# Turning SwiGLU activations on VectorE and through SBUF transfers in place of TensorE

## The chip, the cores and the metric

One core of one Trainium2 chip runs the whole program in one launch. The metric is device time in microseconds. In the text PE is TensorE, DVE is VectorE, ACT is ScalarE, POOL is GpSimd and SP is SyncE, which here only issues DMAs.

## The reference, cut to what matters

A block of a streaming encoder for 256 tokens of width 2048, all in float32: a feed-forward network (SwiGLU, hidden width 5632), a mixer (a state-space branch and a sparse attention branch), and a second feed-forward network of the same shape. The change touches only the second network:

```python
def _swiglu(x, w1, w3, w2):
    return (jax.nn.silu(x @ w1) * (x @ w3)) @ w2

h = h + 0.5 * g3[:, None, :] * _swiglu(hn, ffn2_w1[l], ffn2_w3[l], ffn2_w2[l])
```

`hn` comes from an RMS norm and a modulation by nine vectors, which are slices of `silu(c) @ w_ada`. The last of these slices, the gate g3, is computed while the second network runs.

## The kernel before, in words

**Units.** Every weight is streamed from HBM in units of 256 rows by 512 columns (`raw`, 512 KB, a ring of four). ACT copies a unit into a rounded high part (`cast`, L880, `w_hi`), DVE subtracts to get the low part (`sub`, L1368, `w_lo`), both in rings of four, and PE runs `unit` (L2149): 12 matmuls of 512 columns, for two halves of tokens, two slices of 128 rows and three products (high by high, low by high, high by low).

**Blocks.** The hidden width is cut into 11 blocks of 512 columns. In the steady state (`hidden`) a block has 24 units, called unit 0 to unit 23 here: eight of w1 for the next block, eight of w2 for this block (four quarters of the output, two units each), eight of w3 for the next block. The second network begins with 24 units of mixed order, then `second` (16 units, the block o = 0), then `hidden` for o = 1, three trips of a loop over two blocks each (o = 2 to 7), `hidden` for o = 8, and a closing part with o = 9 and 10.

**The activation of a block.** PE leaves x @ w1 and x @ w3 in PSUM with tokens on the partitions. ACT takes the silu (`silu`), DVE multiplies (`prod`, L1588, at unit 2) into `act_tok`. The product with w2 needs the hidden columns on the partitions, so PE turns `act_tok` with eight 128x128 transposes into PSUM (`turn_act`, L2176, just before unit 5). ACT copies that out as `aT_hi` (`act_hi`, L979, after its cast of unit 7), DVE subtracts to get `aT_lo` (`act_lo`, L1590, after its subtraction of unit 7), and PE uses both from unit 8 on.

**What sets the order.** Every engine's stream is written out by hand and runs in order; semaphores tie them together. SP's order is one load per unit (`load_unit`, L650, which waits until DVE has subtracted the unit four before it). During units 20 to 58 of the second network, SP also loads 32 pieces of `w_ada` (512 KB each, `load_ada`, L656), four for every five units, and DVE adds each into `ada_acc` (`ada_add`, L1376, L1388) right after the subtraction of the unit with which it was loaded; after the 16th and the 32nd piece DVE folds the sum (`fold`, L1395, four transposes and four reductions). In this stretch lie `second` (units 24 to 39, called block 0 here) and the first `hidden` (from unit 40, called block 1). DVE also adds each output quarter into `y` (`y_add`, L1595).

Of the kernel before, what the change touches and what calls it, by code (L numbers as in the profile page):

```python
# [26 lines left out]
ALU = mybir.AluOpType  # L27
# [32 lines left out]
FOLD = 32  # L60
FOLD_COLS = 256
LOOP_FROM = (4, 2)
TRIPS = tuple((FBLK - 1 - o) // 2 - 1 for o in LOOP_FROM)
ADA_MIX = ADA_FIRST + ADA_PEELED[0] + ADA_TRIP * (TRIPS[0] + 1)
ADA_MIXED = 3
# [50 lines left out]
def build(nc, x, c, positions, w_ada, b_ada, norm_ffn1, ffn1_w1, ffn1_w3, ffn1_w2, norm_mix, w_in,  # L116
# [77 lines left out]
    act_tok = place("act_tok", at_temp + 24 * KB, [HALF, NB])  # L194
    aT_hi = place("aT_hi", at_temp + 28 * KB, [4, T], F32R)
    aT_lo = place("aT_lo", at_temp + 32 * KB, [4, T], F32R)
    aT2_hi = place("aT2_hi", at_temp + 56 * KB, [4, T], F32R)
    aT2_lo = place("aT2_lo", at_temp + 60 * KB, [4, T], F32R)
    norm_tmp = place("norm_tmp", at_temp + 20 * KB, [2, 2, T])
# [99 lines left out]
    silu_ready = sem("silu_ready")  # L299
    prod_ready = sem("prod_ready")  # L300
    act_turned = sem("act_turned")
    ahi_ready = sem("ahi_ready")
    alo_ready = sem("alo_ready")
    y_added = sem("y_added")
# [194 lines left out]
    def set_of(m):  # L499

        return max(e for e in range(SETS) if SET_START[e] <= m)

    BLOCK = 3 * UPB
    SECOND = 2 * UPB
    PEELED = (len(EARLY), FIRST + SECOND + BLOCK)
# [7 lines left out]
    def rows_cols(w, row, cols):  # L513

        return w[row:row + 2 * P, cols].rearrange("(k p) n -> p k n", p=P)

    def span(start, size):
        return slice(start, start + size) if isinstance(start, int) else bass.ds(start, size)
# [123 lines left out]

    as2 = lambda t: t.rearrange("p (k n) -> p k n", k=2)

    block = ctx.enter_context(nc.Block())


    @block.sync
    def _(sp):
# [6 lines left out]
        def load_ada(m, source):  # L656
# [2 lines left out]
                sp.wait_ge(ada_used, free)  # L659
            sp.dma_start(ada_row(slot), source).then_inc(ada_in[slot], 16)  # L660


        sp.dma_start(h[:], x[0].rearrange("(s p) d -> p s d", p=P)).then_inc(x_in, 16)
        for u in range(LATE[0]):
# [3 lines left out]
        for f in range(2):  # L668
# [5 lines left out]
            for u, source in enumerate(peeled):  # L674
                if f or u >= LATE[0]:
                    load_unit(At(n + u), source)
                i = ada_unit_after(f, u)
                if i is not None:
                    e, k = divmod(i, KT)
                    e += (ADA_FIRST, ADA_FFN2)[f]  # L680
                    if f and i == 0:
                        sp.wait_ge(unit_done, n)
                    load_ada(At(e * KT + k), ada_source(e, k))
            with sp.Fori(0, TRIPS[f]) as trip:
                pair_of_blocks = [source for e in range(2) for source in ffn_sources(f, False, trip * 2 + (LOOP_FROM[f] + e))]
                for u, source in enumerate(pair_of_blocks):
                    load_unit(At(n + PEELED[f] + u, BODY, trip), source)
                    k = ada_unit_after("trip", u)
                    if f == 0 and k is not None:
                        e = ADA_FIRST + ADA_PEELED[0]  # L690
                        load_ada(At(e * KT + k, ADA_TRIP * KT, trip), ada_source(trip * ADA_TRIP + (e + k // KT), k % KT))
            pair_of_blocks = ffn_sources(f, False, FBLK - 3) + closing_sources(f)
            for u, source in enumerate(pair_of_blocks):
                load_unit(At(n + PEELED[f] + TRIPS[f] * BODY + u), source)
                k = ada_unit_after("trip", u)
                if f == 0 and k is not None:
                    e = ADA_MIX - ADA_TRIP + k // KT
                    load_ada(At(e * KT + k % KT), ada_source(e, k % KT))
            if f == 1:
                break  # L700
            for n in range(MIX, M0):
# [146 lines left out]
    def _(act):  # L848
# [126 lines left out]
        def silu(o, bank=0):  # L975
            act.wait_ge(prod_ready, o.count()) if o.n0 else None
            nc.scalar.activation(silu_a[:], psum[:, bank:bank + HALF, :], ACT.Silu).then_inc(silu_ready, 1)

        def act_hi(o, bank=4, dst=aT_hi):  # L979
            act.wait_ge(act_turned, o.count(plus=1))  # L980
            nc.scalar.activation(dst[:], psum[:, bank:bank + 2, :].rearrange("p b (k t) -> p (b k) t", k=2),
                                 ACT.Copy).then_inc(ahi_ready, 1)

# [25 lines left out]
        def ffn(f):  # L1009
            n0 = ffn_base[f]  # L1010
            o0 = f * FBLK
            if f == 0:
                early()
            else:
                cast_units(n0 + W1_DONE + LAG)
                act.wait_ge(unit_done, n0 + W1_DONE)
                silu(At(o0))

            def second(n, o):

                for u in range(SECOND):
                    cast_units(n.n0 + u + 1)
                    if u == 4:
                        act.wait_ge(unit_done, n.n0)
                        silu(o + 1, FIRST_BANK[2])
                    if u == 7:
                        act_hi(o, 0)

            def hidden(n, o):

                for u in range(BLOCK):
                    if n.per:
                        cast(n + u)
                    else:
                        cast_units(n.n0 + u + 1)
                    if u == 7:
                        act_hi(o)
                    if u == UPB - 1 + LAG:
                        act.wait_ge(unit_done, (n + UPB).count())
                        silu(o + 1)  # L1040

            if f:
                second(At(n0 + FIRST), At(o0))
                hidden(At(n0 + FIRST + SECOND), At(o0 + 1))
            with act.Fori(0, TRIPS[f]) as trip:
                for e in range(2):
                    hidden(At(n0 + PEELED[f] + e * BLOCK, BODY, trip), At(o0 + LOOP_FROM[f] + e, 2, trip))
            done[0] = n0 + PEELED[f] + TRIPS[f] * BODY
            hidden(At(done[0]), At(o0 + FBLK - 3))
            n, o = done[0], o0 + FBLK - 2  # L1050
            for u in range(2 * UPB):
                cast_units(n + u + 1)
                if u == 7:
                    act_hi(At(o))
                if u == UPB - 1 + LAG:
                    act.wait_ge(unit_done, n + UPB)
                    silu(At(o + 1))
            n += 2 * UPB
            cast_units(n + 5)
            act_hi(At(o + 1), 0, aT2_hi)  # L1060
            cast_units(n + 6)
            gate_copy(2 * f)
            if f == 1:
                cast_units(n + 2 * UPB)
                return
            close_tail(1, n)
# [295 lines left out]
    def _(dve):  # L1362
# [219 lines left out]
        def prod(o, n, bank=2):  # L1582

            dve.wait_ge(unit_done, n.count())
            dve.wait_ge(silu_ready, o.count(plus=1))
            if o.n0:
                dve.wait_ge(act_turned, o.count())
            nc.vector.tensor_tensor(act_tok[:], silu_a[:], psum[:, bank:bank + HALF, :], ALU.mult).then_inc(prod_ready, 1)  # L1588

        def act_lo(o, bank=4, hi=aT_hi, lo=aT_lo):  # L1590
            dve.wait_ge(ahi_ready, o.count(plus=1))
# [50 lines left out]
        def ffn(f):  # L1642
# [10 lines left out]
            def second(n, o, adds):  # L1653

                for u in range(SECOND):
                    sub_units(n.n0 + u + 1)
                    ada_peeled(f)
                    if u == 2:
                        prod(o, n)
                    if u == 7:  # L1660
                        act_lo(o, 0)
                    if u == 10:
                        prod(o + 1, n + UPB, 4)
                    if u in (12, 14):
                        q = (u - 12) // 2
                        y_add(adds + q, q, n + (UPB + 2 * q + 2), SECOND_BANKS)
# [12 lines left out]
            def hidden(n, o, adds, w0=0, ada=None, after_second=False):  # L1679


                for u in range(BLOCK):
# [10 lines left out]
                        y_add(At(Y_ADDS[f] + q), q, n + (2 * q + 2 - UPB), SECOND_BANKS)  # L1693
                    if u == 2 and not after_second:
                        prod(o, n)
                    if u == 7:
                        act_lo(o)
                    if u in (12, 14, 16, 18):
                        q = (u - 12) // 2
                        y_add(adds + q, q, n + (UPB + 2 * q + 2))  # L1700
# [14 lines left out]
            for u in range(2 * UPB):  # L1715
# [2 lines left out]
                    later_set(BLOCK + u, piece)  # L1718
                if u == 2:
                    prod(At(o), At(n))  # L1720
                if u == 7:
                    act_lo(At(o))
            n += 2 * UPB
            sub_units(n + 2)
            prod(At(o + 1), At(n))
# [419 lines left out]
    def _(pe):  # L2145
# [199 lines left out]
        def ffn(f):  # L2345
# [12 lines left out]
            def second(n, o, adds):  # L2358

                for u in range(UPB):  # L2360
                    if u == 5:
                        turn_act(o, 0)
                    unit(n + u, xT_hi, xT_lo, 2 * u, 4, u == 0, u == UPB - 1)
                for q in range(QB):
                    if q == 0:
# [9 lines left out]
            def hidden(n, o, adds, after_second=False):  # L2375
# [3 lines left out]
                if after_second:  # L2379
                    pe.wait_ge(y_added, (adds + -2).count())  # L2380
                for u in range(UPB):
                    if u == 5:

                        if adds.n0:
                            pe.wait_ge(y_added, adds.count())
# [2 lines left out]
                for q in range(QB):  # L2388
                    bank = 6 if q % 2 == 0 else 4
                    if q == 0:  # L2390
                        pe.wait_ge(alo_ready, o.count(plus=1))
                    if q >= 2:
                        pe.wait_ge(y_added, (adds + (q - 1)).count())
                    for k in range(2):
# [16 lines left out]
            n, o, adds = n + BLOCK, o + 1, adds + QB  # L2411
            pe.wait_ge(silu_ready, o + 1)
            for u in range(UPB):
                if u == 5:
                    pe.wait_ge(y_added, adds)
                    turn_act(At(o))
                unit(At(n + u), xT_hi, xT_lo, 2 * u, 0, u == 0, u == UPB - 1)
# [3 lines left out]
            for i, (block, q) in enumerate(CLOSING):  # L2421
                last = block == FBLK - 1
                hi, lo = (aT2_hi, aT2_lo) if last else (aT_hi, aT_lo)
                if i == 0:
                    pe.wait_ge(alo_ready, o + 1)
                if i == 1:
                    turn_act(At(o + 1), 0)
                    sum_folds(2 * f, 3)
# [334 lines left out]
```

## Time and profile before

| | us |
|---|---|
| median of three runs | 2528.01 |
| the three runs | 2526.07, 2528.01, 2530.00 |
| span of the profiled execution | 2528.3 |
| PE busy | 2499.9 |
| DVE busy | 1830.6 |
| ACT busy | 1159.0 |

No time of its own is given for the profiled execution beside its span; the span is taken for it. A duration in the trace is from an instruction's start to its recorded end; matmuls overlap, so for PE the distance between starts is what counts. DVE and ACT instructions overlap by about 0.1 us as well. DMA issues are shown on the queue of the engine that issues them (SPq, ACTq).

### The profile page before, as it was taken

Reading aid. Unit: us, or ns where it says so; the run is one execution under the profiler, and the core shown is the slowest. Engines: PE = TensorE matmul, PEld = TensorE weight load, DVE = VectorE, ACT = ScalarE, POOL = GpSimd, SP = SyncE. Lnnn points to the kernel's source line nnn. Section 1 sums busy time; section 2 is a strip of 40 time slices with the busy share of each in tenths; the row PEclk is TensorE's granted clock in tenths of the full one; section 3 lists DMA queues with packets and bytes.
Section 4 is the critical chain, followed back from the end, with each engine's and each line's share of the span. In section 5 each row is a group of like instructions: output and inputs, shape, how many; then the busy total and the mean of one; then the engine's idle time right before and its main releaser. Section 6 shows DMA issues by size and latency. Waiting matters only on the chain.

```text
span 2528.3 us, 33298 instructions
## 1 busy us (share of the span) xinstructions
PE 2499.9 (99%) x12314; PEld 2108.9 (83%) x12314; DVE 1830.6 (72%) x2016; ACT 1159.0 (46%) x1396; POOL 84.0 (3%) x118
## 2 busy tenths in 40 slices
PE   7999999999999999999999999999999999999999
PEld 5778888888888999898888888888888888888887
DVE  6876668898877888887866677776689555555556
ACT  4444444444445555655555444444544444444443
POOL 4210000000000000000100000000000000000000
PEclk9999999999999999999999999999999999999999
DMA  9976579898976777874544778787598655565565
GB/s 370 366 282 194 184 261 344 291 341 291 340 259 210 270 261 268 279 228 152 164 142 138 245 267 272 251 298 243 167 334 301 203 192 190 189 191 188 190 191 173
DMA packets 281219, 614.45 MB, mean 243 GB/s; under 512 B 23586, under 2 KB 24196, under 8 KB 280196
## 3 DMA queue, kind: packets, MB, share of 16 engines
q1 hardware_dynamic: 269600, 571.41, 67.4%
q0 software_dynamic: 9744, 36.73, 3.9%
q10 hardware_dynamic: 1748, 4.62, 0.5%
q8 instruction: 80, 1.31, 0.2%
q14 instruction: 47, 0.39, 0.0%
HBM read 608.43 MB, written 4.25 MB: 242 GB/s over the span
## 4 chain that ended last, share of the span: by engine, by line
PE 95%; DVE 2%; DMA 1%; issue 0%; ACT 0%; ACTq 0%; DVEq 0%
PE psum L2159 27%; PE psum L2161 27%; PE psum L2160 27%; PE psum L2453 3%; PE psum L2455 3%; PE psum L2454 3%; PE psum L2476 2%; PE psum L2147 2%; DMA raw<-in_ffn_w 1%; DVE w_lo L1368 1%; PE psum L2269 0%; DVE ada_acc L1482 0%; DMA badas<-in_b_ada 0%; PE psum L2240 0%; PE psum L2201 0%
## 5 line engine op out<-in xcount | busy, mean ns | idle before, releaser
L1368 DVE TENSOR_TENSOR w_lo<-raw,w_hi 128x1024 fp32r<-128x1024 f32 x850 | 1036.6, 1223 | 518.8 <-ACT w_hi L880 517.6
L880 ACT ACTIVATE w_hi<-raw 128x1024 fp32r<-128x1024 f32 x850 | 899.0, 1060 | 1017.4 <-PE psum L2161 873.5
L2159 PE MATMUL psum<-w_hi,xT_hi 128*128 128x512 f32 x1984 | 784.8, 396 | 6.4 <-issue 4.6
L2161 PE MATMUL psum<-w_hi,xT_lo 128*128 128x512 f32 x1984 | 773.8, 390 | 0.0
L2160 PE MATMUL psum<-w_lo,xT_hi 128*128 128x512 f32 x1984 | 773.5, 390 | 0.0
L2159 PEld LDWEIGHTS psum<-w_hi,xT_hi 128*128 128x128 f32 x1984 | 373.1, 188 | 89.8 <-issue 13.1
L2161 PEld LDWEIGHTS psum<-w_hi,xT_lo 128*128 128x128 f32 x1984 | 372.9, 188 | 78.9
L2160 PEld LDWEIGHTS psum<-w_lo,xT_hi 128*128 128x128 f32 x1984 | 373.2, 188 | 75.8
L2159 PE MATMUL psum<-w_hi,aT_hi 128*128 128x512 f32 x704 | 274.8, 390 | 0.0
L2161 PE MATMUL psum<-w_hi,aT_lo 128*128 128x512 f32 x704 | 274.1, 389 | 0.0
L2160 PE MATMUL psum<-w_lo,aT_hi 128*128 128x512 f32 x704 | 274.0, 389 | 0.0
L1388 DVE SCALAR_TENSOR_TENSOR ada_acc<-ada_raw,cact,ada_acc 128x1024 f32<-128x1024 f32 x210 | 268.9, 1280 | 0.0
L2453 PE MATMUL psum<-xT_hi,w_hi 128*128 128x256 f32 x640 | 182.2, 285 | 0.1
L2455 PE MATMUL psum<-xT_hi,w_lo 128*128 128x256 f32 x640 | 181.1, 283 | 0.0
L2454 PE MATMUL psum<-xT_lo,w_hi 128*128 128x256 f32 x640 | 181.1, 283 | 0.0
L2161 PEld LDWEIGHTS psum<-w_hi,aT_lo 128*128 128x128 f32 x704 | 132.1, 188 | 27.6
L2159 PEld LDWEIGHTS psum<-w_hi,aT_hi 128*128 128x128 f32 x704 | 132.2, 188 | 27.4
L2160 PEld LDWEIGHTS psum<-w_lo,aT_hi 128*128 128x128 f32 x704 | 132.2, 188 | 27.2
L1604 DVE TENSOR_TENSOR y<-psum,y 128x1024 f32<-128x1024 f32 x89 | 108.8, 1222 | 22.2 <-PE psum L2161 22.2
L2453 PEld LDWEIGHTS psum<-xT_hi,w_hi 128*128 128x128 f32 x640 | 122.8, 192 | 0.5 <-issue 0.5
L2454 PEld LDWEIGHTS psum<-xT_lo,w_hi 128*128 128x128 f32 x640 | 122.8, 192 | 0.0
L2455 PEld LDWEIGHTS psum<-xT_hi,w_lo 128*128 128x128 f32 x640 | 122.8, 192 | 0.0
(260 smaller groups left out, 1904.6 us busy)
## 6 DMA issues: line engine op xcount, KB each, us to landing
raw<-in_ffn_w SPq DMA_DIRECT2D x528, 512.0 KB, 4.5
ada_raw<-in_w_ada SPq DMA_DIRECT2D x224, 512.0 KB, 5.7
raw<-in_w_in SPq DMA_DIRECT2D x224, 512.0 KB, 3.8
ada_raw<-in_w_ada POOLq DMA_DIRECT2D x32, 512.0 KB, 7.4
ada_more<-in_w_ada POOLq DMA_DIRECT2D x32, 512.0 KB, 7.3
raw<-in_w_br_ssd SPq DMA_DIRECT2D x32, 512.0 KB, 5.3
raw<-in_w_br_att SPq DMA_DIRECT2D x32, 512.0 KB, 4.5
raw<-in_w_out SPq DMA_DIRECT2D x32, 512.0 KB, 5.1
```

The costliest lines, as they stand in the source:

```text
L880: nc.scalar.activation(w_hi[:, n.slot(SPLIT), 0:size], raw[:, n.slot(RAW), 0:size], ACT.Copy).then_inc(hi_ready, 1)
L1368: nc.vector.tensor_tensor(w_lo[:, n.slot(SPLIT), 0:size], raw[:, n.slot(RAW), 0:size], w_hi[:, n.slot(SPLIT), 0:size], ALU.subtract).then_ ...
L1388: nc.vector.scalar_tensor_tensor(out=acc[:], in0=src, scalar=cact[:, k:k + 1], in1=acc[:], op0=ALU.mult, op1=ALU.add).then_inc(ada_used, 1)
L1604: nc.vector.tensor_tensor(y[:, :, cols], psum[:, bank:bank + HALF, :], y[:, :, cols], ALU.add).then_inc(y_added, 1)
L2147: return nc.tensor.transpose(dst, src, ident[0:rows_, 0:rows_])
L2159: nc.tensor.matmul(o, hi[:, kt + k, toks], whi, start=a, stop=False)
L2160: nc.tensor.matmul(o, hi[:, kt + k, toks], wlo, start=False, stop=False)
L2161: ins = nc.tensor.matmul(o, lo[:, kt + k, toks], whi, start=False, stop=b)
L2453: nc.tensor.matmul(o, w_hi[:, s, cols], xT_hi[:, kt + k, :], start=a, stop=False, skip_group_check=True)
L2454: nc.tensor.matmul(o, w_hi[:, s, cols], xT_lo[:, kt + k, :], start=False, stop=False, skip_group_check=True)
L2455: ins = nc.tensor.matmul(o, w_lo[:, s, cols], xT_hi[:, kt + k, :], start=False, stop=b, skip_group_check=True)
L2476: return nc.tensor.matmul(o, a, b, start=first, stop=last)
```

## The change: what it does

For the blocks o = 0 to 9 of the second network PE no longer turns the activations. DVE transposes `act_tok` in 32x32 pieces within each group of 32 partitions (`turn_bands`, two instructions, one for each half of the tokens), right after `prod`. SP waits for that and issues 16 transfers from SBUF to SBUF, 32 partitions by 1 KB each (`move_act`), which carry each 32-partition band to its place. In SP's stream they stand after the loads of unit 6. ACT and DVE then split `aT_raw` into high and low parts as before, each in two instructions (`moved_hi`, `moved_lo`), at the places where `act_hi` and `act_lo` stood. In the first network and in the last block nothing changes.

```diff
+BLOCKED_FROM = (10, 0)
+BLOCKED = tuple(FBLK - 1 - o for o in BLOCKED_FROM)
+BANDS = P // 32
+BAND_DMAS = BANDS * BANDS
...
+    MOVE_AFTER = 6
...
+        def move_act(o):
+
+            sp.wait_ge(act_blocked, moves_before(o).count(plus=1))
+            for band in range(BANDS):
+                for to in range(BANDS):
+                    sp.dma_start(aT_raw[32 * to:32 * (to + 1), band, :],
+                                 act_blk[32 * band:32 * (band + 1), to, :]).then_inc(act_moved, 16)
...
                 for u, source in enumerate(pair_of_blocks):
...
+                    if blocked(o) and u % BLOCK == MOVE_AFTER:
+                        move_act(o)
...
+        def moved_hi(o, n):
+
+            act.wait_ge(act_moved, moves_before(o).count(plus=1) * 16 * BAND_DMAS)
+            act.wait_ge(unit_done, n.count())
+            for half in range(HALF):
+                ins = nc.scalar.activation(by_tokens(aT_hi, half), by_bands(half), ACT.Copy)
+            ins.then_inc(ahi_ready, 1)
...
+        def turn_bands(o):
+
+            dve.wait_ge(prod_ready, o.count(plus=1))
+            for half in range(HALF):
+                ins = nc.vector.transpose(act_blk[:].rearrange("p c (k s t) -> p s k c t", s=HALF, t=32)[:, half],
+                                          act_tok[:, half, :].rearrange("p (k c t) -> p k c t", c=BANDS, t=32))
+            ins.then_inc(act_blocked, 1)
+
+        def moved_lo(o):
+
+            dve.wait_ge(ahi_ready, o.count(plus=1))
+            for half in range(HALF):
+                ins = nc.vector.tensor_tensor(by_tokens(aT_lo, half), by_bands(half), by_tokens(aT_hi, half), ALU.subtract)
+            ins.then_inc(alo_ready, 1)
...
                     if u == 2:
                         prod(o, n)
+                        turn_bands(o)
                     if u == 7:
-                        act_lo(o, 0)
+                        moved_lo(o)
...
             def second(n, o, adds):
 
                 for u in range(UPB):
-                    if u == 5:
-                        turn_act(o, 0)
...
-                    if u == 5:
+                    if u == 5 and not blocked(o):
 
                         if adds.n0:
                             pe.wait_ge(y_added, adds.count())
...
                         pe.wait_ge(alo_ready, o.count(plus=1))
+                        if blocked(o) and adds.n0:
+                            pe.wait_ge(y_added, adds.count())
```

## Rows read from the trace of the kernel before

**Rows 1.** The page's first and fourth parts: busy time of PE, chain by engine.
```profile
PE 2499.9 (99%) x12314; PEld 2108.9 (83%) x12314; DVE 1830.6 (72%) x2016; ACT 1159.0 (46%) x1396; POOL 84.0 (3%) x118
PE 95%; DVE 2%; DMA 1%; issue 0%; ACT 0%; ACTq 0%; DVEq 0%
```

**Rows 2.** Two stretches of the second network: length, busy us by engine, PEclk, DMA share, GB/s.
```profile
1873.00:1960.00 87.00, 87.00 (x392) 72.19 (x391) 81.62 (x82) 36.84 (x35) 0.00 (x0) 1.00 0.86 307
...
2050.00:2460.00 410.00, 410.00 (x1836) 340.06 (x1835) 224.05 (x186) 170.89 (x163) 0.00 (x0) 1.00 0.60 190
```

**Rows 3.** Timeline of PE, one block behind the loads of w_ada: start, duration, instruction.
```profile
2101.79 0.39 PE L2159 MATMUL psum<-w_hi,xT_hi 128*128 128x512 f32 x1
...
2115.16 0.39 PE L2161 MATMUL psum<-w_hi,xT_lo 128*128 128x512 f32 x1
2115.39 1.03 PE L2147 MATMUL psum<-ident,act_tok 128*128 128x128 f32 x8
...
2116.50 0.40 PE L2160 MATMUL psum<-w_lo,xT_hi 128*128 128x512 f32 x1
```

**Rows 4.** Timelines of DVE and ACT in the same block.
```profile
2102.17 1.22 DVE L1588 TENSOR_TENSOR act_tok<-silu_a,psum 128x1024 f32<-128x1024 f32 x1 [0.58 <-PE psum L2161]
2103.31 1.22 DVE L1368 TENSOR_TENSOR w_lo<-raw,w_hi 128x1024 fp32r<-128x1024 f32 x1
...
2112.87 1.06 ACT L880 ACTIVATE w_hi<-raw 128x1024 fp32r<-128x1024 f32 x1 [1.66 <-PE psum L2161]
```

**Rows 5.** DVE's transposes in 32x32 pieces, line 1406.
```profile
L1406 DVE STREAM_TRANSPOSE fold_tmp<-ada_acc x56: 435/440/450, 416.2 to 1951.9; 128x256 f32<-128x256 f32 x56
```

**Rows 6.** Timeline of ACT's DMA queue: shortest, longest, first and last of four small loads.
```profile
6.97 0.97 ACTq L853 DMA_DIRECT2D vecs<-in_ssd_norm  x1
...
9.05 0.23 ACTq L853 DMA_DIRECT2D vecs<-in_k_norm  x1
...
186.25 0.46 ACTq L886 DMA_DIRECT2D a_exp<-in_ssd_a_log  x1
...
187.71 0.46 ACTq L892 DMA_DIRECT2D pos_col<-in_positions  x1
```

**Rows 7.** SP's loads, line 654: 2050 to 2500 us, then landing in 1810 to 1950.
```profile
L654 SPq DMA_DIRECT2D raw<-in_ffn_w x162: 367/373/382, 2053.9 to 2498.0; - x162
DMA to landing us min/median/max: 3.3/4.3/7.0
...
DMA to landing us min/median/max: 3.4/5.4/8.5
```

**Rows 8.** Timeline of DVE in block 0.
```profile
1860.28 1.22 DVE L1588 TENSOR_TENSOR act_tok<-silu_a,psum 128x1024 f32<-128x1024 f32 x1
...
1868.36 1.23 DVE L1368 TENSOR_TENSOR w_lo<-raw,w_hi 128x1024 fp32r<-128x1024 f32 x1 [1.07 <-ACT w_hi L880]
...
1871.09 1.23 DVE L1368 TENSOR_TENSOR w_lo<-raw,w_hi 128x1024 fp32r<-128x1024 f32 x1 [0.30 <-ACT w_hi L880]
...
1874.59 1.23 DVE L1592 TENSOR_TENSOR aT_lo<-psum,aT_hi 128x1024 fp32r<-128x1024 f32 x1 [1.08 <-ACT aT_hi L981]
```

**Rows 9.** Timeline of DVE from the end of block 0 through block 1.
```profile
1898.58 2.35 DVE L1368 TENSOR_TENSOR w_lo<-raw,w_hi 128x1024 fp32r<-128x1024 f32 x2
...
1907.30 1.22 DVE L1604 TENSOR_TENSOR y<-psum,y 128x1024 f32<-128x1024 f32 x1
...
1920.81 1.22 DVE L1368 TENSOR_TENSOR w_lo<-raw,w_hi 128x1024 fp32r<-128x1024 f32 x1
...
1924.70 1.23 DVE L1368 TENSOR_TENSOR w_lo<-raw,w_hi 128x1024 fp32r<-128x1024 f32 x1 [0.34 <-ACT w_hi L880]
...
1928.12 1.23 DVE L1368 TENSOR_TENSOR w_lo<-raw,w_hi 128x1024 fp32r<-128x1024 f32 x1 [1.01 <-ACT w_hi L880]
...
1953.87 4.62 DVE L1368 TENSOR_TENSOR w_lo<-raw,w_hi 128x1024 fp32r<-128x1024 f32 x4
```

**Rows 10.** Timeline of PE: the first matmul of block 1.
```profile
1903.27 0.39 PE L2159 MATMUL psum<-w_hi,xT_hi 128*128 128x512 f32 x1
```

More of the change, by code:

```diff
@@ L196, in build @@
     aT_lo = place("aT_lo", at_temp + 32 * KB, [4, T], F32R)
+    act_blk = place("act_blk", at_temp + 64 * KB, [BANDS, UNIT // BANDS])
+    aT_raw = place("aT_raw", at_temp + 68 * KB, [BANDS, UNIT // BANDS])
     aT2_hi = place("aT2_hi", at_temp + 56 * KB, [4, T], F32R)
@@ L301, in build @@
     act_turned = sem("act_turned")
+    act_blocked = sem("act_blocked")
+    act_moved = sem("act_moved")
     ahi_ready = sem("ahi_ready")
@@ L515, in rows_cols, with blocked, moves_before, turns @@
         return w[row:row + 2 * P, cols].rearrange("(k p) n -> p k n", p=P)
+    def blocked(o):
+        f, i = divmod(o.n0, FBLK)
+        return BLOCKED_FROM[f] <= i < FBLK - 1
+    def moves_before(o):
+        f = o.n0 // FBLK
+        return o + (-BLOCKED_FROM[0] if f == 0 else BLOCKED[0] - FBLK - BLOCKED_FROM[1])
+    def turns(o):
+        before = sum(1 for i in range(o.n0) if not blocked(At(i)))
+        return At(before) if blocked(o) else o + (before - o.n0)
     def span(start, size):
@@ L643, in build, with by_tokens, by_bands @@
     as2 = lambda t: t.rearrange("p (k n) -> p k n", k=2)
+    def by_tokens(t, half):
+        return t[:, :, half * P:(half + 1) * P].rearrange("p k (b t) -> p k b t", t=32)
+    def by_bands(half):
+        return aT_raw[:].rearrange("p b (k s t) -> p s k b t", s=HALF, t=32)[:, half]
     block = ctx.enter_context(nc.Block())
@@ L683, in _ @@
                     load_ada(At(e * KT + k), ada_source(e, k))
+                for i, at in enumerate((FIRST, FIRST + SECOND)):
+                    if f and u == at + MOVE_AFTER:
+                        move_act(At(f * FBLK + i))
             with sp.Fori(0, TRIPS[f]) as trip:
@@ L691, in _ @@
                         load_ada(At(e * KT + k, ADA_TRIP * KT, trip), ada_source(trip * ADA_TRIP + (e + k // KT), k % KT))
+                    o = At(f * FBLK + LOOP_FROM[f] + u // BLOCK, 2, trip)
+                    if blocked(o) and u % BLOCK == MOVE_AFTER:
+                        move_act(o)
             pair_of_blocks = ffn_sources(f, False, FBLK - 3) + closing_sources(f)
@@ L698, in _ @@
                     load_ada(At(e * KT + k % KT), ada_source(e, k % KT))
+                o = At(f * FBLK + FBLK - 3 + u // BLOCK)
+                if blocked(o) and u % BLOCK == MOVE_AFTER:
+                    move_act(o)
             if f == 1:
@@ L977, in silu @@
             nc.scalar.activation(silu_a[:], psum[:, bank:bank + HALF, :], ACT.Silu).then_inc(silu_ready, 1)
+        def moved_hi(o, n):
[4 more added lines that the diff above has]
+            ins.then_inc(ahi_ready, 1)
         def act_hi(o, bank=4, dst=aT_hi):
-            act.wait_ge(act_turned, o.count(plus=1))
+            act.wait_ge(act_turned, turns(o).count(plus=1))
             nc.scalar.activation(dst[:], psum[:, bank:bank + 2, :].rearrange("p b (k t) -> p (b k) t", k=2),
@@ L1026, in second @@
                     if u == 7:
-                        act_hi(o, 0)
+                        moved_hi(o, n)
             def hidden(n, o):
@@ L1036, in hidden @@
                     if u == 7:
-                        act_hi(o)
+                        moved_hi(o, n) if blocked(o) else act_hi(o)
                     if u == UPB - 1 + LAG:
@@ L1053, in ffn @@
                 if u == 7:
-                    act_hi(At(o))
+                    moved_hi(At(o), At(n)) if blocked(At(o)) else act_hi(At(o))
                 if u == UPB - 1 + LAG:
@@ L1585, in prod @@
             dve.wait_ge(silu_ready, o.count(plus=1))
-            if o.n0:
-                dve.wait_ge(act_turned, o.count())
+            if o.n0 and not blocked(o + -1):
+                dve.wait_ge(act_turned, turns(o).count())
             nc.vector.tensor_tensor(act_tok[:], silu_a[:], psum[:, bank:bank + HALF, :], ALU.mult).then_inc(prod_ready, 1)
+        def turn_bands(o):
[9 more added lines that the diff above has]
+            ins.then_inc(alo_ready, 1)
         def act_lo(o, bank=4, hi=aT_hi, lo=aT_lo):
@@ L1695, in hidden @@
                         prod(o, n)
+                    if u == 2 and blocked(o):
+                        turn_bands(o)
                     if u == 7:
-                        act_lo(o)
+                        moved_lo(o) if blocked(o) else act_lo(o)
                     if u in (12, 14, 16, 18):
@@ L1720, in ffn @@
                     prod(At(o), At(n))
+                    if blocked(At(o)):
+                        turn_bands(At(o))
                 if u == 7:
-                    act_lo(At(o))
+                    moved_lo(At(o)) if blocked(At(o)) else act_lo(At(o))
             n += 2 * UPB
@@ L2413, in ffn @@
             for u in range(UPB):
-                if u == 5:
+                if u == 5 and not blocked(At(o)):
                     pe.wait_ge(y_added, adds)
@@ L2425, in ffn @@
                     pe.wait_ge(alo_ready, o + 1)
+                    if blocked(At(o)):
+                        pe.wait_ge(y_added, adds)
                 if i == 1:
```

## The prediction, written before the change was run

> **What bounds the kernel now.** I read the page's busy line and the chain of waits first. The reader is to see that PE is busy for 99% of the span and makes 95% of the chain [rows 1]: whatever PE no longer does is time, as long as nothing makes it wait. Then two stretches of the second network [rows 2]. From 2050 to 2460 us PE is busy all the time, DVE 55%, ACT 42%, the DMA engines 60%: there is room beside PE. From 1873 to 1960 us, where w_ada is loaded too, DVE is busy 81.62 of 87 us and DMA 0.86 of the time. PE does not wait there either, but there is hardly room for more. The granted clock is 1.00 in both, the 2.4 GHz level, and the change gives no reason for another: PE keeps running.
>
> **What is removed.** A unit takes PE (2115.39 - 2101.79) / 5 = 2.72 us; two matmuls start 0.227 us apart. Around the eight transposes, the second matmul behind them starts at 2116.50, where 2115.16 + 2 x 0.227 = 2115.61 would be due without them [rows 3]. So they cost 0.89 us, less than the 1.03 us that the row records for them, since matmuls overlap. Ten blocks: **-8.9 us**. All of it lies on PE's path.
>
> **What is added on DVE.** The nearest row is the transpose of 128x256 in 0.44 us [rows 5]; 1024 columns of another operation take 1.22 us [rows 4], which makes 1.0 ns a column and 0.18 fixed. A half of 128x512 lies between one such transpose (0.44) and two (0.88); I take 0.70. The next instruction starts 0.08 us before the last one's end [rows 4], but the first transpose waits for prod's end. From prod's start: transposes at 1.25 and 1.87, end at 2.57, the next subtraction at 2.49 in place of 1.14, so 1.35 us later. The low part in two halves costs 0.1 more. 1.45 us a block (0.9 to 1.8).
>
> **What is added on SP, the term that decides.** SP waits for the transposes, then issues 16 transfers before the load of unit 7. No row shows such an issue. A lone load of 512 KB takes 0.37 us [rows 7]; four small loads in a row on ACT's queue take 0.46 us each and start 0.49 apart (187.71 - 186.25 over three) [rows 6], so a small one is not cheaper. The shortest issue seen took 0.23 us, the longest 0.97, both at the start, while other queues load as well [rows 6]; these are the two ends, and with 0.97 the 16 would take 15.5 us. I take 0.49, the rows of the same pattern on an otherwise steady queue: 16 x 0.49 = 7.84 us in which no weight is loaded. Behind the wait on SP stands every later load, and for these wait ACT's casts, then DVE, then PE. The transfers themselves have until the cast of unit 7 and land beside the load behind them. The Trainium skill has another price: DMA: Bandwidth & Descriptors, section Anatomy of one DMA, SWDGE (gpsimd) path, gives about 50 ns for the sequencer's dispatch of a DMA. That is for GpSimd's path, and the rows show nine times as much; by it SP would be held for 0.8 us, and the sum would be near the first rival's.
>
> **The eight plain blocks (2 to 9).** Time from unit 0 on PE (2101.79). prod starts at 0.38 [rows 3, 4], the transposes are done at 2.95, the load of unit 7 is issued at 3.0 + 7.84 = 10.8. It lands 3.3, 4.3 or 7.0 us later (least, median, most [rows 7]); the queue has run empty by then, so I expect 3.3 to 4.3: 15.1. The cast (1.06) and subtraction (1.23) end at 17.4. PE wants unit 7 at 7 x 2.72 = 19.0: **1.6 us spare**. Before, the cast of unit 7 started at 11.1, so this is where 4 us of slack go. The high part, in two halves of at most 0.6 us each, takes ACT until 17.4, the low part DVE until 18.7, and the subtraction of unit 8 ends at 19.9, wanted at 21.8. The loads of units 8 to 10 follow 0.49 apart, and SP has caught up by unit 11. Cost 0; if a landing takes above 5.9 us, what is over. The new wait for y_added before unit 8 is three units later than the old one before unit 5: nothing.
>
> **Blocks 0 and 1, where w_ada is loaded.** Here DVE's lateness carries on. Block 1 begins on PE at 1903.27 [rows 10], so block 0 at 1903.27 - 16 x 2.72 - 0.89 = 1858.9.
> - Block 0: prod at 1860.28 [rows 8], transposes done at 1862.9, load of unit 7 at 1870.75, landed (3.4, the least of this stretch [rows 7], since the queue is empty) at 1874.15, cast until 1875.2. DVE was free at 1870.9 and idles for 4.35 us, where before it idled 1.07 + 0.30 + 1.08 [rows 8]. Subtraction, w_ada piece (1.2) and low part follow, and unit 8 is 3.1 us later than before. Some 0.5 us of small gaps are won back. Then come the 16th piece and the fold, the point at which DVE was latest before: the subtraction of unit 15 ended at 1899.8 [rows 9], and PE wanted it at 1900.55. Now it ends at 1902.4, wanted at 1899.66: PE waits **2.7 us**.
> - Block 1 starts on PE at 1905.1. DVE's addition of unit 2 is at 1907.30 + 2.6 [rows 9], the transposes end at 1912.4, the subtraction of unit 3 at 1913.5, wanted at 1913.25: **0.3**. The load of unit 7 is issued at 1920.3, landed at 1923.7, subtracted at 1926.0, wanted at 1924.4: **1.6**. With a w_ada piece and the low part between, unit 8 ends at 1929.6, wanted at 1928.7: **0.9**. DVE is now 7.6 us late against before (1928.4 for 1920.81 [rows 9]) and wins back 0.34 + 1.01 of idle. At the last fold, unit 19 ended at 1955.05 and was wanted at 1955.86; now 1961.25, wanted at 1955.86 - 1.78 + 5.5 = 1959.6: **1.65**.
> Together PE waits 7.1 us. With the stretch's later landings (4.3 in place of 3.4) it is 8.9; each 0.1 us more or less per issue moves it by 3.2; the bounds of the transposes by 1 either way.
>
> **The sum.** -8.9 + 7.1 = -1.8 against the profiled execution's 2528.3, which is 0.3 above the median of the runs shown: **2526.5 us**, or 0.07% less. A measurement of this kernel tells about 0.2%, 5 us, from no change. So the forecast is: most of what PE gains in ten blocks is lost in two.
>
> **Rivals.**
> 1. *The gain comes through.* If an issue takes 0.23 us, the lower end, the load of unit 7 is 4.2 us earlier and DVE hardly waits for it; DVE's own 1.45 us fit into the idle 2.45 of block 0, and in block 1 only unit 3 is late: it ended at 1909.66, now 1911.2, wanted at 1910.5, 0.7 us. -8.9 + 0.7: **2520.1**. For it: a lone issue is shorter than one in a row [rows 6, 7], and SP is not ACT. At 0.40 us per issue the loss is 4.2 and the time 2523.6. Against: four issues in a row agree to 0.01 us.
> 2. *The loads are late in all blocks.* One mechanism: the stop of SP's queue eats the spare 1.6 us of the plain blocks. It decides from 7.84 + 1.6 = 9.4 us for the 16 transfers, 0.59 us each (or landings above 5.9). At 0.65 us: 1.0 us in each of eight blocks, and 7.1 + 2 x 2.6 = 12.3 in blocks 0 and 1: -8.9 + 8 + 12.3 = +11.4, **2539.7**. For it: 16 outstanding transfers behind one another are shown nowhere, and landings of 7.0 occur. Against: it takes a fifth more than the rows' 0.49. At the upper end of 0.97 the spare time would be overrun by 6.1 us a block and the time be near 2590; I give that 0.03.
> 3. *Between:* 0.49 us per issue, but landings at the medians in both stretches, the transposes at their upper bound: 7.1 + 1.8 + 1 = 9.9, a net +1.0: 2529.3, slower but not measurably.
>
> **How the numbers follow.** The forecast and what lies within 5 us of the time before, rival 3 included: 0.47. Rival 1 down from 0.38 us per issue: 0.33. Rival 2 and its like: 0.20, the upper end's 0.03 included. The range reaches to the first rival's end and halfway to the second's: 2519.5 to 2534.
>
> **What would show it.** Transposes of 128x512 near 0.70 us. SP's 16 issues spanning 7.8 us, and the load of unit 7 at 10.8 us behind unit 0. In the plain blocks ACT's cast of unit 7 waits for a DMA at about 15 us, PE not at all, and a block takes 24 x 2.72 = 65.3 us. PE waits for w_lo in two places of each of the blocks 0 and 1, some 7 us in all, where it hardly waited before. The prediction is wrong if the issues are not 0.45 to 0.55 us apart, or if PE waits in the plain blocks.

## The result, and the profile after

| | before | after |
|---|---|---|
| median, us | 2528.69 | 2542.45 |
| runs, us | 2526.07 to 2530.00 (4) | 2539.79 to 2544.06 (4) |
| profiled execution: time, span | 2530.00, span 2528.3 | 2539.79, span 2538.1 |

Ratio 1.0055, 95% interval 1.0041 to 1.0069: the changed kernel is slower by 0.55%, 13.8 us. The forecast was 2526.5, the range ended at 2534. In every run for which both are known the span is 1.7 us shorter than the time, so the profiled execution of the kernel before is its slowest run, 2530.00, and that of the changed kernel is its fastest. The two profiles therefore differ by only 9.8 us.

PE's and DVE's busy time and the chain by engine on the page, which answer to [rows 1]:

```profile
PE 2495.9 (98%) x12234; PEld 2100.3 (83%) x12234; DVE 1841.8 (73%) x2046; ACT 1158.4 (46%) x1406; POOL 83.8 (3%) x118
PE 85%; DVE 5%; SPq 4%; DMA 3%; issue 2%; ACT 1%; ACTq 0%; DVEq 0%
PE psum L2236 23%; PE psum L2238 23%; PE psum L2237 23%; SPq L700 4%; PE psum L2532 3%; PE psum L2534 3%; PE psum L2533 3%; DMA raw<-in_ffn_w 3%; PE psum L2555 2%; PE psum L2224 2%; DVE w_lo L1425 2%; DVE ada_acc L1445 1%; ACT w_hi L929 1%; DVE act_tok L1645 0%; PE psum L2346 0%
```

PE is busy 4.0 us less, only 1.5 of it in the second network (729.27 and 727.75). The 8.9 us of transposes are gone, but matmuls at half clock, of which more below, count as busy longer. And the chain now runs through SP's queue: L700, the line that issues the transfers, has 4% of it, 100 us, which is ten blocks of 10 us.

The pieces that were added (name, engine, operation, count, ns min/median/max, first and last start):

```profile
L700 SPq DMA_DIRECT2D aT_raw<-act_blk x160: 512/590/1528, 1859.9 to 2454.9; - x160
L1651 DVE STREAM_TRANSPOSE act_blk<-act_tok x20: 668/688/712, 1858.5 to 2444.8; 128x512 f32<-128x512 f32 x20
L1033 ACT ACTIVATE aT_hi<-aT_raw x20: 611/614/617, 1875.3 to 2461.1; 128x512 fp32r<-128x512 f32 x20
L1659 DVE TENSOR_TENSOR aT_lo<-aT_raw,aT_hi x20: 682/684/689, 1877.8 to 2462.4; 128x512 fp32r<-128x512 f32 x20
```

The transposes take 0.69 us (forecast 0.70). An issue takes 0.59, and in a plain block SP stands at its transfers for 10 us. SP's and ACT's timelines in the block that begins on PE at 2112.23:

```profile
2109.47 3.09 SPq L686 DMA_DIRECT2D raw<-in_ffn_w  x2
2115.12 10.04 SPq L700 DMA_DIRECT2D aT_raw<-act_blk  x16
2125.46 0.38 SPq L686 DMA_DIRECT2D raw<-in_ffn_w  x1
```

```profile
2129.18 1.06 ACT L929 ACTIVATE w_hi<-raw 128x1024 fp32r<-128x1024 f32 x1 [7.53 <-DMA raw<-in_ffn_w]
2130.15 1.14 ACT L1033 ACTIVATE aT_hi<-aT_raw 128x512 fp32r<-128x512 f32 x2
2131.80 1.06 ACT L929 ACTIVATE w_hi<-raw 128x1024 fp32r<-128x1024 f32 x1 [0.52 <-DMA raw<-in_ffn_w]
```

SP reaches the transfers 2.9 us behind PE's unit 0, as forecast, and the load of unit 7 13.2 us behind it, where 10.8 was forecast. ACT waits 7.53 us for that load and casts at 16.9; with the cast (1.06) and DVE's subtraction (1.23) the unit is ready at 19.2, and PE wanted it at 19.0. The spare time is gone, by a little.

In blocks 0 and 1 it is more than a little. Who waited for whom from 1850 to 1982 us (engine, line, released by: us in all, times, longest):

```profile
ACT w_hi L929 <- DMA raw<-in_ffn_w: 57.0, 28, 11.2
DVE w_lo L1425 <- ACT w_hi L929: 24.8, 13, 8.2
...
PE psum L2236 <- DVE w_lo L1425: 9.7, 5, 3.8
PE psum L2236 <- DVE y L1676: 1.4, 1, 1.4
```

Read from top to bottom they are one chain: the load is late, so ACT, so DVE, so PE. PE is held up before units 7, 8, 12 and 15 of block 0 (some 2.0, 0.9, 1.6 and 2.5 us) and before units 7 and 19 of block 1 (some 4.1 and 1.6). PE's timeline at the end of block 0 shows what else happened (the first two rows; then block 1 begins), and two windows give the granted clock (length, busy us of PE, PEld, DVE, ACT, POOL, then PEclk, DMA share, GB/s):

```profile
1903.52 0.50 PE L2236 MATMUL psum<-w_hi,aT_hi 128*128 128x512 f32 x1 [2.20 <-DVE w_lo L1425]
...
1904.92 0.63 PE L2237 MATMUL psum<-w_lo,aT_hi 128*128 128x512 f32 x1
...
1907.96 0.40 PE L2236 MATMUL psum<-w_hi,xT_hi 128*128 128x512 f32 x1
```

```profile
1904.10:1907.50 3.40, 3.40 (x10) 2.62 (x9) 3.40 (x5) 0.00 (x0) 0.00 (x0) 0.50 0.84 276
1931.40:1934.80 3.40, 3.40 (x10) 2.62 (x9) 3.40 (x5) 1.31 (x2) 0.00 (x0) 0.50 1.02 392
```

PE waited 2.2 us for a low part, and soon after it went on its clock was granted at 0.50 (1.2 GHz) for 3.4 us: matmuls start 0.43 us apart in place of 0.227. The same follows the longest wait of block 1, 3.8 us. Each stretch costs 1.7 us more. Before, the clock was 1.00 in this stretch [rows 2]. The four runs of the changed kernel differ in this: their mean clocks are 0.998, 0.997, 0.997 and 0.996 as their times rise from 2539.79 to 2544.06, and the profiled one is the fastest.

**Where the time went**, measured on PE from first matmul to first matmul. A plain block of 24 units needs 65.28 us and block 0 with 16 units 43.52, when nothing waits and nothing is turned. 1855.86, 1907.96, 1980.68, 2046.48 and 2112.23 are the starts of block 0, block 1 and the first three plain blocks.

| us | before | after | after, lost to waits and half clock |
|---|---|---|---|
| block 0 | 44.41 | 52.10 | 8.6 |
| block 1 | 66.17 | 72.72 | 7.4 |
| plain block, mean of seven | 66.17 | 66.00 | 0.7 |
| from unit 0 of block 9 to the last unit | 87.21 | 86.65 | 0.3 |
| second network, first to last unit | 726.39 | 738.84 | |

The second network is 12.45 us longer: 8.9 us of transposes gone, 21.4 us come, of which the two stretches at half clock are some 3.4 and waits the rest. It began 3.0 us earlier than in the profile before (1790.47 and 1793.47), which is most of why the spans differ by 9.8 us only. The change touches nothing before the second network, and the start of that network scatters from 1790.5 to 1795.8 us over the twelve profiles.

### The profile page after: what moved, and what is told of

Read it like the earlier page. It is cut to its first block, busy times and chain, and to the rows that moved or that the text cites. A ratio compares the mean times of both kernels' runs of the same rounds, so it can differ in the third digit from the quotient of the medians.

```text
span 2538.1 us, 33333 instructions
## 1 busy us (share of the span) xinstructions
PE 2495.9 (98%) x12234; PEld 2100.3 (83%) x12234; DVE 1841.8 (73%) x2046; ACT 1158.4 (46%) x1406; POOL 83.8 (3%) x118
## 3 DMA queue, kind: packets, MB, share of 16 engines
q8 instruction: 80, 1.31, 0.2%
## 4 chain that ended last, share of the span: by engine, by line
PE 85%; DVE 5%; SPq 4%; DMA 3%; issue 2%; ACT 1%; ACTq 0%; DVEq 0%
PE psum L2236 23%; PE psum L2238 23%; PE psum L2237 23%; SPq L700 4%; PE psum L2532 3%; PE psum L2534 3%; PE psum L2533 3%; DMA raw<-in_ffn_w 3%; PE psum L2555 2%; PE psum L2224 2%; DVE w_lo L1425 2%; DVE ada_acc L1445 1%; ACT w_hi L929 1%; DVE act_tok L1645 0%; PE psum L2346 0%
## 5 line engine op out<-in xcount | busy, mean ns | idle before, releaser
L2236 PE MATMUL psum<-w_hi,xT_hi 128*128 128x512 f32 x1984 | 785.0, 396 | 16.3 <-DVE w_lo L1425 11.1
L2236 PEld LDWEIGHTS psum<-w_hi,xT_hi 128*128 128x128 f32 x1984 | 372.9, 188 | 104.0 <-DVE w_lo L1425 15.7
```

The costliest lines, as they stand in the source:

```text
L2236: nc.tensor.matmul(o, hi[:, kt + k, toks], whi, start=a, stop=False)
```

## The experiments

Theory Q, after the result: SP is held by the issue of 16 transfers, and the weights behind them are late. Rival V: DVE's added work overloads the stretch with w_ada. Rival B: the bytes, packets or latency of the transfers slow the weights. The 17.8 us that two of the expectations give for PE's waits in blocks 0 and 1 is 1.8 too high: the time of its own transposes there was counted twice, and the table above has 16.0.

**1. The transfers alone.** The kernel before, with idle transfers.

```diff
+            sp.wait_ge(prod_ready, o.count(plus=1))
+            for band in range(BANDS):
+                for to in range(BANDS):
+                    sp.dma_start(aT_raw[32 * to:32 * (to + 1), band, :],
+                                 h[32 * band:32 * (band + 1), 0, 256 * to:256 * (to + 1)]).then_inc(act_moved, 16)
```

> The kernel before (TensorE still turns, VectorE does nothing more), with 16 transfers of 32 partitions by 1 KB issued by SP at the same place in each of the ten blocks; they copy part of h to where nothing reads it, and ScalarE waits for them before its high part. Theory Q (the queue: SP is held for 16 x 0.63 = 10 us and every weight load behind waits): the transfers start 1.3 us earlier than in the changed kernel and TensorE wants unit 7 0.9 us later, so the plain blocks lose nothing, but blocks 0 and 1 lose most of the 17.8 us that TensorE waits there in the changed kernel: 8 to 14 us slower than before. Rival V (VectorE's added work is what the stretch with w_ada can't hold): 0 to 2 us slower.

Measured: ratio 1.0043 (1.0027 to 1.0058), 2539.25 us. The plain blocks take 66.17 us, as before; block 0 takes 49.19 and block 1 71.85, 10.5 us more together, with the clock at its full level. A loss of this kind is there without any of DVE's added work and without the activation's way through SBUF, so V is not needed for it. It is 10.5 of the 16.0 us of the changed kernel, and two stretches at half clock, 3.4 us, are in the 16.0 alone. Q and B are not told apart by this run.

**2. Four transfers in place of 16, the same bytes.** The pieces are not carried to other partitions, so this kernel does not compute the same.

```diff
-            for band in range(BANDS):
-                for to in range(BANDS):
-                    sp.dma_start(aT_raw[32 * to:32 * (to + 1), band, :],
-                                 act_blk[32 * band:32 * (band + 1), to, :]).then_inc(act_moved, 16)
+            for band in range(BANDS):
+                sp.dma_start(aT_raw[:, band, :], act_blk[:, band, :]).then_inc(act_moved, 16)
```

> The changed kernel with 4 transfers of 128 partitions by 1 KB in place of 16 of 32 partitions: the same bytes, but the pieces are not carried to other partitions (so the activation is left in the wrong order). Theory Q: SP is held for some 2.5 us, the loads of unit 7 are on time, and 6 to 8.5 us come off the time before. Rival B (the bytes and packets of the transfers, or their latency, delay the weights): same bytes, so 10 to 14 us slower than before, as the changed kernel. Rival V: still 3 to 8 us of waits in blocks 0 and 1, so -6 to 0.

Measured: ratio 0.9978 (0.9968 to 0.9987), 2522.75 us, 4.9 below the kernel before that was run beside it (2527.62). All plain blocks take 65.28 us, block 0 43.52, block 1 67.62. So B is out: half a megabyte per block from SBUF to SBUF costs PE nothing when few issues carry it. The gain of 6 to 8.5 was missed by a little; in the profile the second network is 6.3 us shorter. Block 1 still loses 2.3 us, nearly all of it in one wait before unit 19.

```profile
L699 SPq DMA_DIRECT2D aT_raw<-act_blk x40: 471/601/614, 1861.1 to 2429.7; - x40
```

A transfer four times as large costs the same 0.60 us to issue.

**3. The 16 transfers on GpSimd's queue.**

```diff
+        for o in range(FBLK, FBLK + BLOCKED[1]):
+            pool.wait_ge(act_blocked, o - FBLK + 1)
+            for band in range(BANDS):
+                for to in range(BANDS):
+                    pool.dma_start(aT_raw[32 * to:32 * (to + 1), band, :],
+                                   act_blk[32 * band:32 * (band + 1), to, :]).then_inc(act_moved, 16)
         gate(2)
```

> The changed kernel with the same 16 transfers issued by GpSimd, which has nothing else to do there; SP's stream is as before. Theory Q: loads of weights are on time; 16 issues of GpSimd at 0.55 us are 9 us, landed about 14 us behind unit 0 where 17 is still in time: 6 to 8.5 us faster than before. If GpSimd takes over 0.9 us for each, the high part comes too late and the gain is lost in all blocks. Rival B: as the changed kernel, 10 to 14 us slower than before.

Measured: ratio 0.9997 (0.9988 to 1.0006), 2526.76 us: no change from before, some 15 us less than the changed kernel. The plain blocks are all at 65.28 us, so there the theory holds in full. The expected gain failed in blocks 0 and 1, 48.16 and 67.96 us. First the issues and their landing, then the waits from 1850 to 1982 us:

```profile
L880 POOL DMA_DIRECT2D aT_raw<-act_blk x160: 496/496/553, 1860.3 to 2439.4; - x160
...
DMA to landing us min/median/max: 1.7/3.8/6.2
```

```profile
ACT w_hi L918 <- DMA raw<-in_ffn_w: 33.0, 17, 4.4
...
ACT aT_hi L1022 <- DMA aT_raw<-act_blk: 10.9, 2, 5.6
DVE aT_lo L1648 <- ACT aT_hi L1022: 8.4, 2, 4.3
PE psum L2225 <- DVE w_lo L1414: 4.3, 3, 2.2
```

In blocks 0 and 1, where the DMA engines were busy 0.86 of the time already [rows 2], now the transfers are late: up to 6.2 us from issue to landing, and ACT waits 5.6 us for them, with its casts behind. The queue has a part in it: the same transfers land 3.8 us after their issue on GpSimd's queue and 1.9 on SP's in the changed kernel (medians). And the clock: after a wait of 2.2 us in block 0 it is at 0.50 for 3.4 us.

**4. Four transfers behind each of four loads.**

```diff
-        def move_act(o):
+        def move_act(o, part):
 
-            sp.wait_ge(act_blocked, moves_before(o).count(plus=1))
-            for band in range(BANDS):
+            if part == 0:
+                sp.wait_ge(act_blocked, moves_before(o).count(plus=1))
+            for band in (part,):
...
-                    if blocked(o) and u % BLOCK == MOVE_AFTER:
-                        move_act(o)
+                    if blocked(o) and u % BLOCK - MOVE_AFTER in range(BANDS):
+                        move_act(o, u % BLOCK - MOVE_AFTER)
```

> The changed kernel with SP issuing the 16 transfers in four groups of four, behind the loads of units 6, 7, 8 and 9, so that no weight load waits behind more than four (2.5 us). Theory Q: no waits in the plain blocks (-0.88 us each), and in blocks 0 and 1, where SP also issues w_ada pieces, at most 3 us: 5 to 8.5 us faster than before. Rival B: the same bytes and packets at nearly the same time, so 5 us slower or more.

Measured: ratio 1.0027 (1.0016 to 1.0039), 2536.07 us. I missed this one. The plain blocks do what was expected, 65.28 us each; blocks 0 and 1 take 50.63 and 73.82, longer together than in any kernel so far but the changed one. The waits from 1850 to 1982 us:

```profile
ACT aT_hi L1034 <- DMA aT_raw<-act_blk: 19.7, 2, 10.0
...
DVE aT_lo L1660 <- ACT aT_hi L1034: 16.7, 2, 8.4
...
PE psum L2237 <- DVE w_lo L1426: 9.9, 2, 6.2
```

Behind each load there SP also issues a piece of w_ada, so the fourth group comes too late: in block 0 it begins 11.1 us behind the first. ACT waits 10 us for it with all its casts behind. And the half clock comes on top, once in each of the two blocks, for 6.8 us from 1884.0 and from 1935.2 (columns as above):

```profile
1884.10:1890.70 6.60, 6.02 (x14) 4.78 (x15) 6.60 (x7) 1.95 (x3) 0.00 (x0) 0.50 0.71 236
1935.30:1941.90 6.60, 3.88 (x9) 3.13 (x10) 6.46 (x7) 4.80 (x6) 0.00 (x0) 0.50 0.86 306
```

Of the 15.7 us that the two blocks lose, PE's waits are 9.9. Whichever comes last on SP's queue, weights or activation, PE pays for it.

**5 to 7. Blocks 2 to 9 alone.** TensorE turns blocks 0 and 1 again; the transfers on GpSimd's queue, on SP in fours, and on SP as in the change.

```diff
-BLOCKED_FROM = (10, 0)
+BLOCKED_FROM = (10, 2)
...
                     if u == 7:
-                        moved_hi(o, n)
+                        moved_hi(o, n) if blocked(o) else act_hi(o, 0)
```

> As with GpSimd issuing, but only for blocks 2 to 9; blocks 0 and 1 are turned by TensorE as before. Theory Q with what the second network showed so far (a plain block takes 65.28 us when no weight is late, 66.17 with TensorE's transposes): 8 x 0.89 = 7.1 us faster than before, 2521 us. If the transfers disturb anything outside the plain blocks, or GpSimd's descriptors slow the weights: less than 4.

> SP issues four transfers behind each of the loads of units 6 to 9, only for blocks 2 to 9. Theory Q: the plain blocks are at 65.28 us as in the run with all ten blocks, and the 14 us lost in blocks 0 and 1 are not there: 7.1 us faster than before, 2521 us.

> The change as it is (16 transfers in a row on SP), only for blocks 2 to 9. Theory Q: blocks 0 and 1 are as before and the plain blocks give what the changed kernel's did, 65.7 to 66.7 us in place of 66.17: 1 to 3 us faster than before, within 0.2%. If blocks 0 and 1 only handed their lateness on, the plain blocks give more, up to 7.

| kernel | ratio (interval) | median, us | block 0, 1 | plain blocks |
|---|---|---|---|---|
| GpSimd | 0.9982 (0.9973 to 0.9991) | 2524.61 | 44.45, 66.17 | 65.28 |
| SP, fours | 0.9974 (0.9965 to 0.9983) | 2521.53 | 44.41, 66.17 | 65.28, one 65.69 |
| SP, 16 in a row | 0.9994 (0.9985 to 1.0003) | 2526.83 | 44.41, 66.17 | 65.86 to 66.81 |

The kernel before, run beside them: 2529.10. The version with fours beats both kernels, by 7.6 us against before: the whole gain of eight blocks. GpSimd's version keeps 4.5; its profile has 2 us of waits at the very end. They are not behind the transfers, the last of which was issued by 2437.1 us, but behind the gate's way through GpSimd's queue. ACT copied `gate_rows` by 2479.8 us and GpSimd sent it on only at 2483.12, 3.3 us later; in experiment 3 and in the version with fours it took 0.3. DVE then waited for `gate_ffn`, the factor on y, 3.8 us, and 1.3 in the version with fours:

```profile
DVE y L1822 <- DMA gate_ffn<-gate_rows: 3.8, 1, 3.8
```

Why GpSimd was late, and whether that makes the 3.1 us between the two medians, no run shows. The third row shows the edge from the other side: with 16 in a row the plain blocks lose as much to late weights as they gain, although blocks 0 and 1 are on time, so this loss is not handed on from them. PE's waits from 1982 to 2500 us, in that kernel:

```profile
PE psum L2237 <- DVE w_lo L1425: 4.8, 7, 1.2
```

SP's timeline in a block of the version with fours, with no PE wait in the same stretch:

```profile
2101.00 2.44 SPq L701 DMA_DIRECT2D aT_raw<-act_blk  x4
2103.70 0.37 SPq L686 DMA_DIRECT2D raw<-in_ffn_w  x1
2104.12 2.41 SPq L701 DMA_DIRECT2D aT_raw<-act_blk  x4
2106.81 0.38 SPq L686 DMA_DIRECT2D raw<-in_ffn_w  x1
```

Loads are 3.1 us apart for four units, where PE uses one in 2.72; 1.6 us of lateness, and there is more than that to spare.

**8. VectorE's transposes alone.**

```diff
                     if u == 2:
                         prod(o, n)
+                        turn_bands(o)
```

> The kernel before with VectorE's two 32x32 transposes added behind prod in the ten blocks; nobody reads them, TensorE turns as before. Theory Q: nothing in the plain blocks, at most 2.5 us in blocks 0 and 1: 0 to 2.5 us slower. Rival V: much of the 17.8 us that TensorE waits in blocks 0 and 1 of the changed kernel, 6 us slower or more.

Measured: ratio 1.0000 (0.9991 to 1.0009), 2528.62 us. Blocks 0 and 1 take 44.41 and 66.17 us, to the last digit as before. DVE's 1.35 us per block fall wholly into its idle time. V is out as the cause by itself. That the added work costs nothing beside a held SP is not shown: the 2.3 us that block 1 lost in experiment 2 had both, and no run takes them apart.

**9. Eight transfers more.**

```diff
+            for band in range(2):
+                for to in range(BANDS):
+                    sp.dma_start(spare[32 * to:32 * (to + 1), band, :],
+                                 act_blk[32 * band:32 * (band + 1), to, :]).then_inc(act_moved, 16)
```

> The changed kernel with eight more transfers of the same kind in each block, issued right behind the 16 and written where nothing reads them. Theory Q: SP is held for 24 x 0.63 = 15.1 us in place of 10.1; a plain block, which had just run out of spare time at 10.1, loses the whole difference of 5.0 us and takes 70.5 to 71.5 us in place of 65.9; with blocks 0 and 1 some 50 us slower than the changed kernel, 2590 us. Rival B (bytes and packets): half as many bytes again, 1 us or less a block, 5 to 8 us in all, 2550 us.

Measured: ratio 1.0315 (1.0298 to 1.0332), 2610.11 us; the plain blocks take 72.6 to 74.1 us, mean 73.5. B is out by a factor of ten. Q's sign and order hold, but its size was short: 7.5 us more per plain block than in the changed kernel, not 5.0. SP's timeline, then a window in a plain block:

```profile
2145.75 10.03 SPq L701 DMA_DIRECT2D aT_raw<-act_blk  x16
2155.82 5.02 SPq L705 DMA_DIRECT2D spare<-act_blk  x8
```

```profile
2091.40:2098.10 6.70, 3.06 (x7) 2.48 (x8) 4.31 (x5) 4.64 (x6) 0.00 (x0) 0.50 0.98 332
```

The hold is 15.1 us as computed. What was left out is the clock: it stands at 0.50 for 6.8 us in every plain block and for 10.2 in blocks 0 and 1. Not all of that costs, as PE is busy only 3.06 of these 6.7 us; in a plain block some twelve matmuls start 0.43 us apart in place of 0.227, which is about the missing 2.5 us.

**10. The source in HBM.** Experiment 1 with `x[0]` in place of `h`, run once.

> The first of these experiments (the kernel before with 16 idle transfers) with x in HBM as the source in place of h in SBUF, same shape of 32 partitions by 1 KB. It measures one issue: if it is the SBUF source that makes an issue cost 0.63 us in place of the 0.49 of the small loads on ScalarE's queue, 0.49 here; if it is the shape or SP's queue, 0.63 again. Time about as in the first experiment or 4 us less.

```profile
L684 SPq DMA_DIRECT2D aT_raw<-in_x x160: 310/421/1846, 1859.1 to 2444.4; - x160
```

```profile
2106.84 7.31 SPq L684 DMA_DIRECT2D aT_raw<-in_x  x16
```

The 16 issues take 7.3 us, 0.46 apart, where the same shape out of SBUF takes 10.0, 0.63 apart. Same queue, same 32 partitions by 1 KB: the source makes the difference. The one run took 2533.62 us, 5.6 less than the median of experiment 1. Blocks 0 and 1 take 46.20 and 70.25 us, 3.0 and 1.6 less than there; SP is held 2.8 and 1.4 us less in them. So in this stretch PE loses about as much more as SP is held longer.

## Why the prediction was wrong, by its own steps

- **What bounds the kernel, what is removed: right.** A plain block without a late weight is 65.28 us long (forecast 65.3), 0.89 less. Ten blocks give the 8.9 us.
- **What is added on DVE: right.** 0.69 us a transpose, the second ending 1.31 us behind the first one's start. It costs nothing by itself (experiment 8).
- **What is added on SP: the term that failed.** "I take 0.49, the rows of the same pattern" [rows 6]. Those rows were loads from HBM. A transfer out of SBUF starts 0.63 us behind the last one on SP (the changed kernel, experiments 1 and 9), and the load of unit 7 is issued 10.3 us behind the first of the 16, where 7.84 was forecast. The mechanism, the engines it passes through and its place were right; the size of one issue was not. Out of HBM SP takes 0.46 us (experiment 10), near the 0.49: the rows were of another kind of source.
- **The plain blocks.** The cost was put at zero up to a hold of 9.4 us, and beyond that at what is over. With 10.3 us this gives 0.9 us a block with the forecast's landing of 4.3 us, and 0.5 with the 3.9 that the load of unit 7 took on average; measured 0.7. The rule was right, the number fed to it wrong. 0.7 of the 0.89 us gained goes here.
- **Blocks 0 and 1.** Forecast 7.1 us of waits, measured 16.0. SP was held 10.4 and 11.0 us there, 5.7 more in all than twice 7.84; by the forecast's own slope (3.2 us for each 0.1 us of issue, which is one for one) that makes 5.7 of the 8.9 missing. Two stretches at half clock make 3.4, and these the forecast denied: "the change gives no reason for another". The load of unit 7 in block 0 landed 4.1 us after its issue, not 3.4, which by the forecast's other slope is 1.4. Together 10.5, more than the 8.9: these shares are estimates, and no run takes them apart. Nor did the waits fall where they were forecast. In block 0 PE was to wait at unit 15 alone and was held up at units 7, 8 and 12 too.
- **The rivals.** Rival 2, late loads in all blocks, is what happened in kind, with its threshold of 0.59 us per issue crossed by 0.04. Its case at 0.65 us asked for 1.0 us in each plain block and 12.3 in the others and gave 2539.7; the time is 2542.45. It was given 0.20. Rival 1 needed short issues and had none, but its time, 2520.1, is about what experiments 2 and 6 reached when the hold was cut.
- **The Trainium skill's 50 ns** for the sequencer's dispatch (DMA: Bandwidth & Descriptors, Anatomy of one DMA, SWDGE (gpsimd) path): GpSimd's queue, which that section is about, takes 0.496 us an issue here (experiment 3), ten times as much. The row is of the whole issue and does not show the dispatch apart, so it does not refute the figure; but the price of a row of issues is the whole.
- **What it was measured against.** The -1.8 us were added to 2528.3 as the profiled execution's time. That is its span; its time was 2530.00, 2.0 above the median of the runs shown. This moves the forecast by less than 2 us, and the measured time stays well above it.

Left open: why an issue out of SBUF takes 0.17 us longer, and where the 1.4 us between the second network's difference in the profiles (12.45) and the medians' (13.8) lie. The lower clocks of the slower runs point at more half-clock stretches, but only the fastest run was profiled, and the start of the second network alone scatters by more than that.

## What to carry to other kernels

An in-order queue that streams weights is a resource with a budget: here 2.72 us a unit, of which a load takes 0.4. Count the issues that are put on it, price each by a transfer of the same kind of source, and compare their sum with the slack of what stands behind; bytes and packets may cost nothing at all. Where the sum is over, cut the batch into pieces that fit between the loads, or give it to a queue that is idle, and leave it out where the queue is full anyway.

## What the runs showed of the hardware that was not expected

- A transfer of 32 partitions by 1 KB is issued by SP every 0.63 us out of SBUF and every 0.46 us out of HBM; by GpSimd, out of SBUF, every 0.49. It lands 1.9 us after its issue on SP's queue and 3.8 on GpSimd's (medians). Four times the size (128 partitions) is no dearer: an issue lasts 0.60 us in place of 0.59.
- PE's clock falls to half after some waits: after waits of 2.2 and 3.8 us in the changed kernel for 3.4 us each, which costs 1.7 us each time beside the wait. It is no rule by the wait's length alone: in experiment 1 a wait of the same 2.2 us was followed by none. Nor does the stretch follow the wait in length: it was 3.4 us at the wait of 3.8, and 6.8 us at the waits of 3.7 and 6.2 in experiment 4, where the clock fell before PE went on.
